# One core, hybrid decoder trunk: four of 42 weight units of each 64-slot expert multiplied as plain float32, and a new order of the 64-slot expert jobs

## The reference

```python
def swiglu(x, w_in, w_out):
    gate, up = jnp.split(x @ w_in, 2, axis=-1)
    return (jax.nn.silu(gate) * up) @ w_out

def moe_swiglu(x, router, w_in, w_out):      # 256 tokens, D = 1024, 8 experts of width 3584
    ...
    top_v, top_i = lax.top_k(logits, MOE_TOP_K)
    top_w = jax.nn.softmax(top_v, axis=-1)
    gates = jnp.sum(jax.nn.one_hot(top_i, N_EXPERTS) * top_w[..., None], axis=1)
    for e in range(N_EXPERTS):
        out = out + gates[:, e:e + 1] * swiglu(xt, w_in[e], w_out[e])
```

## Time and profile before

| | |
|---|---|
| median of 3 runs | 1513.35 us (1511.95 to 1513.36) |
| profiled execution | 1512.7 us, of which the span is 1511.0 us |
| mean granted TensorE clock | 0.979 |
| PE busy | 1428.3 us, 95% |
| DVE busy | 1145.6 us, 76% |
| ACT busy | 959.0 us, 63% |
| HBM read | 444.63 MB |

### The profile page before, as it was taken

One profiled execution on the slowest core, in us unless ns is written; L12 is line 12 of the kernel. 1 busy time (PEld: TensorE's weight loads), 2 busy tenths in 40 slices (PEclk: granted clock), 3 DMA queues, 4 the chain that ended last, 5 costly groups with the idle time before them and its releaser, 6 DMA issues.

```text
span 1511.0 us, 18519 instructions
## 1 busy us (share of the span) xinstructions
PE 1428.3 (95%) x7386; PEld 1210.5 (80%) x7386; DVE 1145.6 (76%) x791; ACT 959.0 (63%) x791; POOL 66.6 (4%) x69
## 2 busy tenths in 40 slices
PE   6999999999999899999989998899999889999996
PEld 6987779999899778877778886778887777888885
DVE  3456664444657578898998888899889899889886
ACT  4334544334444457768877777887777887777774
POOL 1001200000000142000001000001000000000000
PEclk9999999999999979999999999999999999999998
DMA  9554556555464459999999999999999999999990
GB/s 348 183 176 158 195 167 219 176 190 194 141 223 167 140 188 362 357 352 366 392 405 368 356 359 361 390 418 366 364 358 349 386 414 400 357 354 378 364 361 30
DMA packets 158695, 446.89 MB, mean 296 GB/s; under 512 B 7040, under 2 KB 45952, under 8 KB 158608
## 3 DMA queue, kind: packets, MB, share of 16 engines
q1 hardware_dynamic: 156784, 439.38, 79.7%
q0 software_dynamic: 1824, 6.33, 1.3%
HBM read 444.63 MB, written 1.05 MB: 295 GB/s over the span
## 4 chain that ended last, share of the span: by engine, by line
PE 78%; ACT 12%; DVE 9%; issue 1%; DMA 1%; DVEq 0%; POOL 0%; SPq 0%; ACTq 0%; POOLq 0%
PE ps L1396 22%; PE ps L1398 21%; PE ps L1397 21%; ACT whi L824 7%; PE ps L1836 3%; PE ps L1799 3%; PE ps L1800 2%; DVE wlo L945 2%; ACT whi_more L824 2%; DVE wlo_more L945 2%; PE ps L1716 1%; PE ps L1793 1%; DVE wlo L377 1%; DMA raw<-in_ret_w_in 1%; ACT up_rows L863 1%
## 5 line engine op out<-in xcount | busy, mean ns | idle before, releaser
L945 DVE TENSOR_TENSOR wlo<-raw,whi 128x2048 fp32r<-128x2048 f32 x209 | 475.0, 2290 | 66.6 <-ACT whi L824 65.8
L824 ACT ACTIVATE whi<-raw 128x2048 fp32r<-128x2048 f32 x208 | 395.9, 1915 | 125.5 <-PE ps L1398 99.1
L377 DVE TENSOR_TENSOR wlo<-raw,whi 128x2048 fp32r<-128x2048 f32 x81 | 185.8, 2294 | 160.9 <-ACT whi L370 160.9
L370 ACT ACTIVATE whi<-raw 128x2048 fp32r<-128x2048 f32 x83 | 158.7, 1912 | 156.5 <-PE ps L1398 151.4
L1396 PE MATMUL ps<-xT_hi,whi 128*128 128x256 f32 x576 | 164.2, 285 | 6.9 <-DVE wlo L377 6.9
L1396 PE MATMUL ps<-whi,xg_big 128*128 128x512 f32 x420 | 166.8, 397 | 0.0
L1398 PE MATMUL ps<-whi,xg_big 128*128 128x512 f32 x420 | 164.6, 392 | 0.0
L1397 PE MATMUL ps<-wlo,xg_big 128*128 128x512 f32 x420 | 164.4, 391 | 0.0
L1398 PE MATMUL ps<-xT_hi,wlo 128*128 128x256 f32 x576 | 163.8, 284 | 0.0
L1397 PE MATMUL ps<-xT_lo,whi 128*128 128x256 f32 x576 | 163.8, 284 | 0.0
L1396 PEld LDWEIGHTS ps<-xT_hi,whi 128*128 128x128 f32 x576 | 111.5, 193 | 7.7 <-issue 7.3
(11 more groups left out here) (251 smaller groups left out, 2761.7 us busy)
## 6 DMA issues: line engine op xcount, KB each, us to landing
raw<-in_moe_w_in SPq DMA_DIRECT2D x168, 1024.0 KB, 6.7
raw<-in_moe_w_out SPq DMA_DIRECT2D x84, 1024.0 KB, 7.0
more_raw<-in_moe_w_in SPq DMA_DIRECT2D x56, 1024.0 KB, 6.7
more_raw<-in_moe_w_out SPq DMA_DIRECT2D x28, 1024.0 KB, 6.8
raw<-in_ret_w_in SPq DMA_DIRECT2D x24, 1024.0 KB, 5.1
raw<-in_ffn_w_in SPq DMA_DIRECT2D x22, 1024.0 KB, 4.9
raw<-in_ffn_w_out SPq DMA_DIRECT2D x11, 1024.0 KB, 4.9
raw<-in_ret_w_out SPq DMA_DIRECT2D x8, 1024.0 KB, 4.8
```

The source lines that it names most:

```text
L370: nc.scalar.activation(whi[:, u % SPLIT, :], src, ACT.Copy).then_inc(hi_done, 1)
L377: nc.vector.tensor_tensor(wlo[:, u % SPLIT, :], src, whi[:, u % SPLIT, :].bitcast(F32), ALU.subtract).then_inc(lo_done, 1)
L824: nc.scalar.activation(moe_split(n)[0], moe_raw(n), ACT.Copy).then_inc(hi_done, 1)
L945: return nc.vector.tensor_tensor(dst, src, hi.bitcast(F32), ALU.subtract)
```

## The change

Four of the 42 units of each small job (numbers 11, 19, 31 and 38, `SMALL_NATIVE`) are not split. TensorE multiplies them as float32 straight from the slot in which they landed: `both` gets `lo = None` and issues one float32 matmul a piece. ACT's and DVE's work on these units goes; the split buffers go round over the split units alone (`splits(n)`); the slot is held until TensorE is done with the unit.

The small jobs have a stream of their own: up 1 now stands ahead of out 0, and up 3 ahead of out 1, so that out 0 starts with unit 16 (12 before) and out 1 with unit 32 (24 before). There are two `gT_small` in place of one. In ACT's loop the copies out of the banks (`small_copies`) stand ahead of `moe_hi(i + 4)`, and both gate banks are copied after the last gate unit. In all jobs behind the first, `scatter(0)` stands after unit 2 (unit 1 before), and DVE's first addition at unit 3 of its loop (unit 2 before).

```diff
+    SMALL_STREAM = [(part, b, q) for part, b in (("gate", 0), ("up", 0), ("gate", 1), ("up", 1), ("out", 0), ("gate", 2),
+                                                 ("up", 2), ("gate", 3), ("up", 3), ("out", 1), ("out", 2), ("out", 3))
+                    for q in range(BLOCK_UNITS[b])]
...
-    SMALL_GATE = BIG_SILU
-    SMALL_GATE_TURN = {5: 0, 13: 1, 25: 2, 34: 3}
-    SMALL_UP = {7: 0, 19: 1, 31: 2, 35: 3}
-    SMALL_UP_TURN = {8: 0, 20: 1, 32: 2, 36: 3}
-    SMALL_MUL = {9: 0, 21: 1, 33: 2, 37: 3}
-    SMALL_LO = {10: 0, 22: 1, 34: 2, 38: 3}
+    SMALL_NATIVE = (11, 19, 31, 38)
+    SMALL_GATE = {3: 0, 11: 1, 23: 2, 29: 3}
+    SMALL_GATE_TURN = {5: 0, 12: 1, 24: 2, 32: 3}
+    SMALL_UP = {7: 0, 15: 1, 27: 2, 31: 3}
+    SMALL_UP_TURN = {8: 0, 16: 1, 28: 2, 33: 3}
+    SMALL_MUL = {9: 0, 17: 1, 29: 2, 34: 3}
+    SMALL_HI = {10: 0, 18: 1, 30: 2, 35: 3}
+    SMALL_LO = {12: 0, 20: 1, 32: 2, 37: 3}
...
+        SPLITS = [n for n in range(MOE_UNITS) if not (SMALL[n // JOB_UNITS] and n % JOB_UNITS in SMALL_NATIVE)]
...
+            def slot_free(n):
...
+                elif native(n - MRAW):
+                    sp.wait_ge(unit_used, U_MOE + n - MRAW + 1)
+                else:
+                    sp.wait_ge(lo_done, U_MOE + splits(n - MRAW) + 1)
...
-                if n < MOE_UNITS:
+                if n < MOE_UNITS and not native(n):
                     moe_landed(act, n)
-                    if n != SPLIT:
-                        act.wait_ge(unit_used, U_MOE + n - (MSPLIT if n > SPLIT else SPLIT) + 1)
+                    order = splits(n)
+                    if order > SPLIT:
+                        act.wait_ge(unit_used, U_MOE + SPLITS[order - MSPLIT] + 1)
...
                 for i in range(JOB_UNITS):
+                    if SMALL[j]:
+                        small_copies(i, u)
                     moe_hi(j * JOB_UNITS + i + MSPLIT)
...
-                        elif i in (2, 5):
-                            t, at = i // 3, 1 + POSITION[j - 1]
+                        elif i in (3, 5):
+                            t, at = i // 5, 1 + POSITION[j - 1]
...
+                if lo is None:
+                    return pe.matmul(dst, a.bitcast(F32), hi, start=start, stop=stop, skip_group_check=True)
...
-                pe.wait_ge(lo_done, u + i + 1)
+                if native(n):
+                    moe_landed(pe, n)
+                else:
+                    pe.wait_ge(lo_done, U_MOE + splits(n) + 1)
...
-                    if j > 0 and i == 1:
+                    if j > 0 and i == 2:
                         pe.wait_ge(selT_ready, j)
                         pe.wait_ge(y_lo_done, 2 * j)
                         scatter(0)
```

More of the change, by code:

```diff
@@ L59, in build @@
     BLOCK_UNITS = [4, 4, 4, 2]
[L60 to L63, removed]
+    BIG_STREAM = [(part, b, q) for part, b in (("gate", 0), ("up", 0), ("gate", 1), ("out", 0), ("up", 1), ("gate", 2),
+                                               ("out", 1), ("up", 2), ("gate", 3), ("up", 3), ("out", 2), ("out", 3))
+                  for q in range(BLOCK_UNITS[b])]
+    SMALL_STREAM = [(part, b, q) for part, b in (("gate", 0), ("up", 0), ("gate", 1), ("up", 1), ("out", 0), ("gate", 2),
+                                                 ("up", 2), ("gate", 3), ("up", 3), ("out", 1), ("out", 2), ("out", 3))
+                    for q in range(BLOCK_UNITS[b])]
+    assert EFF == 3 * W + BANK and len(BIG_STREAM) == len(SMALL_STREAM) == JOB_UNITS and U_MOE % SPLIT == 0 and JOB_UNITS % RAW == 0
     HALF = P // 2
@@ L210, in build @@
         gT_lo, _ = place("gT_lo", [P, 8, P], F32R)
-        gT_small, _ = place("gT_small", [P, 8, P], F32R, at=gT_at)
+        gT_small = [place(f"gT_small{i}", [P, 8, P], F32R, at=gT_at + i * 4096)[0] for i in range(2)]
         sel, _ = place("sel", [P, 2, T, 2 * P], F32R)
@@ L382, in build, with native, splits @@
         U_AGAIN = U_MOE + MOE_UNITS
+        SPLITS = [n for n in range(MOE_UNITS) if not (SMALL[n // JOB_UNITS] and n % JOB_UNITS in SMALL_NATIVE)]
+        S_AGAIN = U_MOE + len(SPLITS)
+        def native(n):
+            return n not in SPLITS
+        def splits(n):
+            return len([i for i in SPLITS if i < n])
         def moe_slot(n):
@@ L858, in small_drains @@
                     nc.scalar.activation(act_small[:, 0:w], ps[:, 0, 0:w], ACT.Silu).then_inc(small_silu, 1)
[L859 to L866, removed]
+                if i in SMALL_HI:
+                    b = SMALL_HI[i]
                     c = 2 * BLOCK_UNITS[b]
@@ L1220, in moe_lo @@
             def moe_lo(n):
-                if n < MOE_UNITS:
+                if n < MOE_UNITS and not native(n):
                     hi, lo = moe_split(n)
-                    dve.wait_ge(hi_done, U_MOE + n + 1)
+                    dve.wait_ge(hi_done, U_MOE + splits(n) + 1)
                     lo_of(lo, moe_raw(n), hi).then_inc(lo_done, 1)
@@ L1326, in small_drains @@
                     w = BLOCK_UNITS[b] * P
+                    if 4 * small + b > 0:
+                        dve.wait_ge(small_lo, 4 * small + b)
                     dve.wait_ge(small_silu, 4 * small + b + 1)
@@ L1751, in pieces, with big_unit @@
                 return [(4 * q + c, 0, c * BANK) for c in range(4)]
-            def big_unit(i, u, big, job, x, hi, lo, before_gate, before_up):
-                part, b, q = STREAM[i]
+            def big_unit(i, ready, big, job, x, hi, lo, before_gate, before_up):
+                part, b, q = BIG_STREAM[i]
                 if q == 0 and part == "gate":
@@ L1824, in small_unit @@
                             w = slice((2 * c + half) * BANK, (2 * c + half + 1) * BANK)
-                            last = both(ps[:, 4 + half, :], gT_small[:, 2 * q + c, :], hi[:, w], lo[:, w],
+                            last = both(ps[:, 4 + half, :], gT_small[b % 2][:, 2 * q + c, :], hi[:, w], lo if lo is None else lo[:, w],
                                         b == 0 and q == 0 and c == 0, b == 3 and q == 1 and c == 1)
```

66 lines of the change are left out of this document (39 added, 27 removed).

## The result

The changed kernel takes 1490.8 us (median of 4 runs, 1489.65 to 1491.39), the kernel before 1513.36 us on the same chip (4 runs): a ratio of 0.9852, 95% interval 0.9835 to 0.9869. The forecast was 1490. The profiled execution has a span of 1487.9 us, 23.1 less than the 1511.0 of before.

A forecast was written before the change was run, and what follows sets the result against it. Small jobs were taken to be bound by TensorE's waits for ACT's copies and DVE's split. Three times 6.6 us from small jobs plus 2.9 from big ones, 22.7 us, gave 1490 us; 8-in-10 range 1481 to 1505.

The forecast's parts named there:

- Float32 records: On TensorE in the four native units: 0.43 us per 512-wide float32 record, so +6.5 us a small job.
- Waits that go: In small jobs, TensorE's waits for bank copies (8.1 us with tails) and for gT_small (4.3 us) go.
- The scatter: At a small job's start, 2.2 us of waiting become 0.4 + 3.3, the latter ahead of scatter(1): 1.5 us lost.
- A small job's sum: TensorE's work 97.6, restarts 1.4, waits 3.7, one half-clock dip 1.6: 104.3 us a small job, against 110.9.
- The wait for y_lo goes: In the four big jobs behind the first, with scatter(0) one unit later: 2.9 us gained in all.
- The DMA step: In small jobs, queue holds lose some 6 us, eating about 7 of some 14 us of lead; cost booked as zero.
- What the native units are for: In small jobs, they take 9.2 us off DVE and 7.7 off ACT, letting TensorE run without pauses, for +6.5 us there.
- rival 1: The DMA side mildly becomes the bound: small jobs of 108 us, 11.6 us gained, 1501 us in all; chance 0.17.
- 2 (DMA): Each of four holds starves SP's DMA queue: small jobs of 121.1 us, 1540 us in all; chance 0.06.
- ACT's splits released by landings: Sign that the forecast is wrong: ACT's splits wait for DMA landings for long; no size was given.
- 5 (no more than 390 GB/s over a whole job): Small jobs already stand at the core's intake ceiling, 385 to 390 GB/s, nothing won there: 1510 us; chance 0.03.
- Rival 4: Copies first only shift the wait onto the split buffers, 1 us at each of eight copies: 1514 us; chance 0.04.

The follow-up runs named there:

- add_early: The changed kernel with DVE's first addition at unit 2 of its loop again, scatter(0) still after unit 2: 1483.2 us, ratio 0.9791 to the kernel before.
- half_dma: The changed kernel, but from unit 8 of a small job on only half of each unit's bytes are loaded: 1486.9 us, ratio 0.9817 to the kernel before.
- no_native_add: The changed kernel without native units and with DVE's first addition at unit 2 of its loop: 1476.8 us, ratio 0.9755 to the kernel before.
- no_native: The changed kernel with no native unit, all 42 units of a small job split: 1485.8 us, ratio 0.9811 to the kernel before.
- native_only: The kernel before plus the four native units and the joint copy of the gate banks, all else old: 1495.4 us, ratio 0.9888.
- native_elsewhere: The kernel before plus four native units at 1, 17, 29 and 40 and the joint gate bank copy: 1504.9 us, ratio 0.9947.
- copies_only: The kernel before with bank copies ahead of split copies and the joint gate bank copy, no native unit, old stream and scatters: 1501.5 us, ratio 0.9928.

## Why the prediction was right, and where not

The time was right, 1490 forecast and 1490.8 measured; the account below it less so, and that the sum came so near is in part luck. It had 19.8 us from the small jobs, 2.9 from the big ones and nothing from elsewhere, 22.7 in all. Measured were 24.0 from the small jobs, 2.4 lost in two big ones and nothing gained behind them, and 1.5 from ahead of the small jobs, where nothing was changed: 23.1. One error of 4.2 us and one of 5.3 nearly cancel. By its steps:

- *Float32 records.* Forecast as 0.43 us each from narrower ones, measured 0.43. The working has a slip: eight records, four of 256 and four of 128 columns, are 1536 columns, so that 1.22 us are 0.79 ns a column and not 0.40; 512 columns at 0.79 are 0.41 us. That a record costs about twice a float32r matmul of its width (0.227 us for 512 columns, 0.44 ns each) is right.
- *Waits that go.* All eleven for copies and gT_small went, as forecast.
- *The scatter.* 3.3 us of idle PE ahead of scatter(1) were forecast from the earlier trace rows, about 3.05 from start to start measured, at the place and by the releaser named; one half-clock stretch a small job, as counted. add_early confirms the step: undoing that one line of DVE's order shortens the small jobs by 2.4 us.
- *A small job's sum* was 104.3, measured 102.7 to 103.2, 1.3 us less. The largest part is the merges: they were priced at 1.81 us from a row behind a wait, and without the wait take 1.70 (the short ones 0.81 in place of 0.91), 0.9 us a job. So the price of a merge held 0.11 us that belonged to the wait ahead of it.
- *The big jobs: the mis-sized term.* "The wait for y_lo goes", 2.9 us of gain. The big jobs behind the first two small ones grew by 2.4 us, and what follows the third kept its 260.1. The DMA step had it that the lead of 14 us would be eaten "with nothing to spare" and booked zero. All of it was eaten, ACT then waits for landings at the start of the big job, so y_lo and the third split ahead of the addition are late, and PE waits 0.2 and 1.1 us at the two scatters. half_dma shows it: with the landings early, that job takes 123.3 us, 1.1 less than before the change, so the gain at y_lo is real and the debt hides it. The debt is 2.2 us for each of the two such jobs, and 1.9 us in what follows the third (258.2 in place of 260.1). Late landings do not make it alone: in add_early ACT waits for them as long, but with the addition behind two splits the big job takes 124.6. What should have been asked of the lead is not only whether the small job gets through on it, but what the next job's start finds.
- *What the native units are for: a wrong reason.* The prediction charged them with 6.5 us a job on TensorE and justified that by DVE's relief, which "lets TensorE run without pauses". The relief is real and does not pay: between add_early and no_native_add the native units save 5.5 us of pauses a small job and cost 6.5. The forecast of the whole change was right because it took both together; had it been asked for the parts, it would have failed, as the expectations of no_native and native_only did. Alone (with the joint copy of the gate banks), the native units gain 18 us; with the new order they lose 5 to 6.4. Both the native units in their places and the new order keep ACT's split copy from standing between the end of a part and its bank copies, and that can be won only once.
- *Rivals.* 1 and 2 (DMA) did not come in the small jobs; the eating of the lead that rival 1 names did, and was paid in the big ones. One sign that the prediction named for being wrong, ACT's splits released by landings, was there: 3.2 and 2.2 us in the first small job. 5 (no more than 390 GB/s over a whole job) did not come: 397 GB/s over the big job behind, 400 over a small job of no_native_add. Rival 4 did not come: no PE wait in the small jobs is released by wlo.

Left open: how much of native_elsewhere's gain over the kernel before (8 us) is DVE's relief and how much the shorter waits at gate merges and y_lo. Nor do the runs show what exactly brings a half-clock stretch: before, there are seven in the small jobs, in the changed kernel three, in add_early and no_native_add none, and in native_elsewhere one, with three waits of 1.22 us before a merge in each job.

## What to carry to other kernels

An engine that works ahead (ACT's split for a unit four later) must not stand in its own queue ahead of work that the critical engine waits for now; in the new order putting the urgent copy first cost TensorE no wait for a split, while buying the same room with slower work on the critical engine cost 6.5 us a job. (In copies_only the wait moved in part to the next step, so the next step has to be given room as well.) Two remedies for one wait do not add up, so each part has to be measured in the company in which it will stand: here the new order is faster without the native units. When one stage gets faster than its supply, ask what the next stage finds: the debt appears there.

## What the runs showed of the hardware

A plain float32 matmul of 128x512 is two records of 0.43 us, 0.86 us in all, against 0.227 us for a float32r one: nearly four times. Loads of 1 MiB came in at 420 GB/s over 25 us on this one core, and the time from issue to landing then told the length of the queue and not the speed of a transfer: 8.8 and 14.6 us with the same 420 GB/s (5.0 us in a big job). A merge of 16 matmuls of 64 columns took 1.70 us in a running TensorE and 1.81 behind a wait. An engine that is busy for 98.1 of 99.6 us was still not all that bound the stage: a change on another engine took 1.2 of the remaining 1.5 us.
